# Constant products on TensorE in its first pauses, and a new order of splits, scans and maxima in the first mixer

## The chip, the cores and the metric

The kernel runs on one core of one Trainium2 chip. The metric is the device time of one execution in microseconds (us); the median of three runs of the kernel before is 1240.11 us.

## What is computed

The reference passes 256 rows of width 1024 through two blocks of two layers each, all in fp32. The change touches the first mixer of the first layer alone:

```python
z = xn @ w_in                              # 256 x 2048: q, k, v, u, 512 columns each
q = partial_rope(q) * 64 ** -0.5; k = partial_rope(k)      # 8 heads of 64
att = dilated_attention(q, k, v)           # causal, three dilated windows joined
bu = einsum('gpc,bsgc->bsgp', b_bar, u)    # S5: complex state input,
h = scan(h[t] = a_bar * h[t-1] + bu[t])    # scan over the 256 rows,
y = einsum('gcp,bsgp->bsgc', c, h).real + d * u            # output and skip
ssm = gelu(y) * sigmoid(gelu(y) @ w_glu)
out = concatenate([att, ssm]) @ w_out
```

Behind it follow a feed-forward layer, a gated recurrence with its own, then a latent attention and a grouped attention, each with attention to a memory and a feed-forward layer.

## The kernel before, in words

**Products.** Every fp32 operand of a large product is split into a rounded part and the rest, both fp32r: "hi" is a rounding copy on ScalarE, "lo" a subtraction on VectorE, and a product is hi·hi + hi·lo + lo·hi, three 128x512 matmuls (`mm3`, lines 484 to 486). Transposes are products with the identity (line 490).

**Weights.** All weights come as chunks of 128x2048 (1 MB) in the order of their use. SP's queue loads them into three raw slots (line 2778; a load waits for the lo split of the chunk three before it). `feed(c)` on ScalarE (split at line 1199) and on VectorE (line 1838) splits the chunks up to c + 3; the split tiles have three slots too, so ScalarE's split of a chunk waits until TensorE has used the chunk three before it. Chunks 0 and 1 are u, 2 and 3 q, 4 and 5 k, 6 and 7 v, 8 the first of the output projection, 9 the GLU, 10 to 12 the rest of the output projection.

**The first edge.** x comes in two row tiles of 512 KB. SP issues the first tile, the identity, chunk 0 in quarters, the second tile, chunks 1 and 2, then the S5 tables (BC with B in one layout, C into YG, B in another layout into BB) and the attention's mask (cbias). TensorE waits for the identity and the first tile, turns it (`turn(0, 0)`), and `first_edge` makes the u products: row tile 0 against the quarters of chunk 0 as they come (lines 529 to 539), the turn of tile 1 in between, then `edge_product` (lines 518 to 521) for tile 1 and for chunk 1. ScalarE and VectorE write the turned tiles as hi and rest (VectorE line 1855).

**The middle.** `rows_mm` runs q, k and v, eight k steps of six matmuls each; its argument `at` names what is put behind a step. `u_turn`, `q_turn`, `k_turn` turn u, q and k; `b_turn` turns B; `b_u(q)` (line 753) makes the state input of block q of four, `c_h(q)` (lines 765 to 774) the output of block q from the products W of scan q, `direct_terms` a small table. VectorE runs, for each block, `rotate` (lines 2198 to 2205, the state input times cosine and sine tables and two subtractions), `scan` (two scans, line 2215, then two products W, lines 2219 and 2220, that `c_h` waits for), `skip` (line 2185) and a `table` step (line 2176), after `late_b` (from line 2153) and `late_c` (from line 2163), which form coefficients; GpSimd forms further ones (from line 2693) as soon as `late_c` is done, and `c_h(0)` waits for them. VectorE's order is written out by hand, with a `feed` between these steps.

**The attention.** `attention0` on TensorE makes the scores of heads 0 and 1, then `c_h(3)`, then goes through the heads: scores of head h + 2 (line 801), the turned exponentials of head h (line 490), the product with V of head h - 1 (line 826). Scores of head h + 2 wait for the maxima of head h, which VectorE makes (line 2281; it also adds the mask), the turn for ScalarE's exponentials (line 1524). Ahead of the first exponential ScalarE copies V (`evac_in`) and runs `feed` for chunk 10. The first product with V waits for `skip(2)`. VectorE puts the feeds of chunks 8, 9 and 10 between the maxima of the heads.

Of the kernel before, what the change touches and what calls it, by code (L numbers as in the profile page):

```python
# [8 lines left out]
NR = 3  # L9
# [211 lines left out]
class Tally:  # L221
# [12 lines left out]
    fills half fin turn hthi htlo x yg sq var rs hi2 rowsq hsq  # L234
# [21 lines left out]
def program(nc, A, PLAN, NCH):  # L256
# [10 lines left out]
    with top:  # L267
# [214 lines left out]
        def pe(e):  # L482
# [39 lines left out]

            def first_edge():

                for i in range(4):
                    w = slice(512 * i, 512 * i + 512)
                    e.wait_ge(S.hthi, htlo_n(0, 0, i))
                    e.wait_ge(S.hi, i + 1)
                    e.matmul(PS[:, 0, :], HTh[:, i, 0:128], WH[:, 0, w], start=i == 0, stop=False)
                    e.wait_ge(S.htlo, htlo_n(0, 0, i))  # L530
                    e.matmul(PS[:, 0, :], HTl[:, i, 0:128], WH[:, 0, w], start=False, stop=False)
                    if i == 1:
                        e.wait_ge(S.c_x1, 16)
                        turn(0, 1, (0,))
                    elif i == 3:
                        turn(0, 1, (1,))
                for i in range(4):
                    e.wait_ge(S.lo, i + 1)
                    e.matmul(PS[:, 0, :], HTh[:, i, 0:128], WL[:, 0, 512 * i:512 * i + 512], start=False, stop=False)
                for k in range(4):  # L540
                    tk = edge_product(0, 0, PS[:, 1, :], 1, k, slice(512 * k, 512 * k + 512))
                tk.then_inc(S.used, 1)
                for t in range(2):
                    for k in range(4, 8):
                        if t == 0 and k == 4:
                            e.wait_ge(S.lo1, 1)
                        elif t == 0 and k == 6:
                            e.wait_ge(S.lo, 5)
                        tk = edge_product(0, 1, PS[:, t, :], t, k, slice(512 * k - 2048, 512 * k - 1536))
                tk.then_inc(S.used, 1)  # L550
# [242 lines left out]
            def attention0():  # L793
# [45 lines left out]
                c_h(3)  # L839
                for h in range(9):  # L840
                    if h + 2 < 8:
                        products(h + 2)
                    if h < 8:
                        turn_p(h)
                    if h:
                        pv(h - 1)
                    if h == 5:
                        finish(0)
# [79 lines left out]

            e.wait_ge(S.c_id, 16)
            e.wait_ge(S.c_x0, 16)  # L930
            turn(0, 0)
            first_edge()
# [262 lines left out]
        def act(e):  # L1195
# [288 lines left out]
            feed(PLAN["ev_u"][1])  # L1484
# [348 lines left out]
        def dve(e):  # L1833
# [257 lines left out]
            pd = Tally()  # L2091
            e.wait_ge(S.pa, PA["DT"])
# [66 lines left out]
            def late_c(then):  # L2159
# [6 lines left out]
                then()  # L2166
# [41 lines left out]
            def scan(q):  # L2208
# [5 lines left out]
                for r in range(2):  # L2214
                    e.tensor_tensor_scan(flat(Gq[:, r, :, :]), flat(RT[:, 4 * q:4 * q + 4, :]), flat(Gq[:, r, :, :]), 0.0, MUL, ADD).then_inc(S.dv, dv.up())  # L2215
                if q:
                    e.wait_ge(S.ch, q)
                e.wait_ge(S.dv, dv.n)
# [40 lines left out]
            def attention0():  # L2259
                def step(h):  # L2260
                    if h == 2:
                        skip(2)
                        skip(3)
                    elif h == 3:
                        feed(PLAN["ev_k"][1])
                    elif h == 5:
                        feed(PLAN["ev_v"][0])
                    elif h == 8:
                        feed(PLAN["ev_v"][1])

                e.wait_ge(S.c_m, 16)
                for h in range(9):
                    step(h)
                    if h < 8:
                        for t in range(2):
                            n = 128 * (t + 1)
                            if t == 0:
                                e.wait_ge(S.qk, h + 1)
                                if h > 1:
                                    e.wait_ge(S.ex, 2 * (h - 2) + 2)  # L2280
                            e.tensor_tensor_reduce(out=SM0[:, h % 2, t, 0:n], in0=PS[:, h % 2, 256 * t:256 * t + n], in1=cbias[:, t, 0:n],
                                                   scale=-1.0, scalar=3e38, op0=ADD, op1=ALU.min, accum_out=M0[:, h, t:t + 1]).then_inc(S.mx, 1)
# [489 lines left out]
        def sync(e):  # L2772
# [21 lines left out]
            for c in range(NR, NCH):  # L2794
                weights(c)
# [57 lines left out]
```

## Time and profile before

| | |
|---|---|
| three runs | 1239.87, 1240.11 (median), 1241.81 us |
| profiled execution | 1240.0 us; span of its instructions 1238.2 us |
| TensorE (PE) | 99% of the span busy |
| VectorE (DVE) | 75% |
| ScalarE (ACT) | 57% |
| GpSimd (POOL) | 7% |
| weights and other reads | 214.5 MB, 174 GB/s over the span |

A row of the timeline gives the start and the length of an instruction, or of several merged ones, in us from the span's start; matmuls overlap, so the distance between two starts, not the length, is the pace. In brackets stands how long the engine stood idle before it, and for whom.

### The profile page before, as it was taken

Reading aid. Unit: us, or ns where it says so; the run is one execution under the profiler, and the core shown is the slowest. Engines: PE = TensorE matmul, PEld = TensorE weight load, DVE = VectorE, ACT = ScalarE, POOL = GpSimd, SP = SyncE. Lnnn points to the kernel's source line nnn. Section 1 sums busy time; section 2 is a strip of 40 time slices with the busy share of each in tenths; the row PEclk is TensorE's granted clock in tenths of the full one; section 3 lists DMA queues with packets and bytes.
Section 4 is the critical chain, followed back from the end, with each engine's and each line's share of the span. In section 5 each row is a group of like instructions: output and inputs, shape, how many; then the busy total and the mean of one; then the engine's idle time right before and its main releaser. Section 6 shows DMA issues by size and latency. Waiting matters only on the chain.

```text
span 1238.2 us, 16107 instructions
## 1 busy us (share of the span) xinstructions
PE 1225.8 (99%) x6318; PEld 1021.4 (82%) x6318; DVE 928.7 (75%) x1293; ACT 705.9 (57%) x1065; POOL 89.3 (7%) x121
## 2 busy tenths in 40 slices
PE   7999999999999999999999999999999999999998
PEld 6778888888888888888888888888888888888887
DVE  7995767698788766778887756676888785666787
ACT  7765654455898644455687535444456644544452
POOL 2410000000100100000232000000001300000000
PEclk9999999999999999999999999999999999999999
DMA  8344545555554565555554224545455315555452
GB/s 308 106 137 148 188 171 204 187 187 203 192 201 159 197 213 197 174 189 212 183 200 170 69 103 169 205 170 204 170 204 187 132 35 204 204 173 199 172 183 89
DMA packets 32539, 216.63 MB, mean 175 GB/s; under 512 B 3904, under 2 KB 4544, under 8 KB 7376
## 3 DMA queue, kind: packets, MB, share of 16 engines
q1 hardware_dynamic: 30384, 210.32, 48.6%
q0 software_dynamic: 1360, 4.78, 1.2%
q8 instruction: 50, 0.82, 0.3%
q10 hardware_dynamic: 720, 0.50, 0.1%
q14 instruction: 25, 0.20, 0.1%
HBM read 214.54 MB, written 1.05 MB: 174 GB/s over the span
## 4 chain that ended last, share of the span: by engine, by line
PE 93%; DVE 4%; issue 1%; DMA 1%; ACT 0%; SPq 0%; DVEq 0%; ACTq 0%
PE PS L484 26%; PE PS L486 26%; PE PS L485 26%; PE PS L490 6%; PE PS L860 2%; PE PS L884 1%; PE PS L521 1%; PE PS L519 1%; PE PS L518 1%; PE PS L567 1%; PE PS L562 1%; PE PS L561 1%; DVE WL L1838 1%; DVE YG L2215 1%; DMA X<-in_x 1%
## 5 line engine op out<-in xcount | busy, mean ns | idle before, releaser
L1838 DVE TENSOR_TENSOR WL<-RAW,WH 128x2048 fp32r<-128x2048 f32 (+3 forms) x200 | 434.1, 2174 | 182.3 <-ACT WH L1199 182.3
L1199 ACT ACTIVATE WH<-RAW 128x2048 fp32r<-128x2048 f32 (+3 forms) x200 | 364.4, 1824 | 262.2 <-PE PS L486 262.1
L484 PE MATMUL PS<-WH,HTh 128*128 128x512 f32 (+1 forms) x848 | 334.6, 395 | 0.8 <-DVE WL L1838 0.6
L486 PE MATMUL PS<-WH,HTl 128*128 128x512 f32 (+1 forms) x848 | 329.0, 388 | 0.0
L485 PE MATMUL PS<-WL,HTh 128*128 128x512 f32 (+1 forms) x848 | 328.3, 387 | 0.0
L486 PEld LDWEIGHTS PS<-WH,HTl 128*128 128x128 f32 x848 | 159.2, 188 | 33.3
L484 PEld LDWEIGHTS PS<-WH,HTh 128*128 128x128 f32 x848 | 159.4, 188 | 32.7 <-DVE WL L1838 1.7
L485 PEld LDWEIGHTS PS<-WL,HTh 128*128 128x128 f32 x848 | 159.5, 188 | 30.6
L484 PE MATMUL PS<-WH,YAh 128*128 128x512 f32 x354 | 139.9, 395 | 0.1
L486 PE MATMUL PS<-WH,YAl 128*128 128x512 f32 x354 | 138.0, 390 | 0.0
L485 PE MATMUL PS<-WL,YAh 128*128 128x512 f32 x354 | 137.8, 389 | 0.0
L486 PEld LDWEIGHTS PS<-WH,YAl 128*128 128x128 f32 x354 | 66.4, 188 | 14.0
L484 PEld LDWEIGHTS PS<-WH,YAh 128*128 128x128 f32 x354 | 66.5, 188 | 13.7 <-issue 0.5
L485 PEld LDWEIGHTS PS<-WL,YAh 128*128 128x128 f32 x354 | 66.5, 188 | 13.0
L2635 POOL TENSOR_SCALAR st<-st 128x2 f32<-128x2 f32 (+4 forms) x33 | 21.0, 636 | 752.5 <-ACT JK L1237 679.7
L1216 ACT ACTIVATE YAh<-PS 128x512 fp32r<-128x512 f32 x38 | 21.7, 588 | 58.2 <-DVE JK L2027 29.2
L1216 ACT ACTIVATE HTh<-PS,cst 128x128 fp32r<-128x128 f32 (+1 forms) x136 | 38.8, 380 | 21.9 <-PE PS L490 21.9
L1855 DVE SCALAR_TENSOR_TENSOR HTl<-PS,cst,HTh 128x128 fp32r<-128x128 f32 (+1 forms) x136 | 38.7, 351 | 10.7 <-ACT HTh L1216 10.6
L484 PE MATMUL PS<-WH,YBh 128*128 128x512 f32 x112 | 43.9, 392 | 0.0
L486 PE MATMUL PS<-WH,YBl 128*128 128x512 f32 x112 | 43.6, 389 | 0.0
L485 PE MATMUL PS<-WL,YBh 128*128 128x512 f32 x112 | 43.6, 389 | 0.0
L1854 DVE TENSOR_TENSOR HTl<-YG,HTh 128x512 fp32r<-128x512 f32 x64 | 39.8, 683 | 0.0
(446 smaller groups left out, 1737.6 us busy)
## 6 DMA issues: line engine op xcount, KB each, us to landing
RAW<-in_w SPq DMA_DIRECT2D x196, 1024.0 KB, 4.9
BC<-in_rows POOLq DMA_DIRECT2D x4, 512.0 KB, 4.1
YG<-in_mem POOLq DMA_DIRECT2D x4, 512.0 KB, 5.0
X<-in_x SPq DMA_DIRECT2D x2, 512.0 KB, 5.4
RAW<-in_w SPq DMA_DIRECT2D x4, 256.0 KB, 5.7
BC<-in_s SPq DMA_DIRECT2D x1, 512.0 KB, 11.6
YG<-in_s SPq DMA_DIRECT2D x1, 512.0 KB, 11.9
BB<-in_s SPq DMA_DIRECT2D x1, 512.0 KB, 12.5
```

The lines of the kernel that those rows point to most:

```text
L484: e.matmul(out, ah, bh, start=start, stop=False, skip_group_check=joined)
L485: e.matmul(out, ah, bl, start=False, stop=False, skip_group_check=joined)
L486: return e.matmul(out, al, bh, start=False, stop=stop, skip_group_check=joined)
L490: return e.transpose(out, src, ident[0:p, 0:p])
L518: e.matmul(out, HTh[:, k, ts], WH[:, c % NW, w], start=k == 0, stop=False)
L860: tk = e.matmul(PS[:, h % 2, 256 * t:256 * t + 256], q[:, 128 * t:128 * t + 128], k[:, 0:256], start=i == 0, stop=i == len(parts) - 1)
L1199: e.activation(WH[:, c % NW, w], RAW[:, c % NR, w], ACT.Copy).then_inc(S.hi, 1)
L1216: return e.activation(out, src, ACT.Copy, scale=scale)
L1838: e.tensor_tensor(WL[:, c % NW, w], RAW[:, c % NR, w], WH[:, c % NW, w].bitcast(f32), SUB).then_inc(S.lo, 1)
L1854: return e.tensor_tensor(out, src, hi.bitcast(f32), SUB)
L1855: return e.scalar_tensor_tensor(out, src, gain, hi.bitcast(f32), MUL, SUB)
L2635: e.tensor_scalar(st[:, at:at + n], st[:, at:at + n], 1e-6, None, ADD).then_inc(S.var, 1)
```

## The change

It has six parts. TensorE gets 14 products on a constant tile (`idle_products`), nine ahead of the first turn and five behind it; VectorE writes the tile first of all. `first_edge` has a new order: all hi and rest products of tile 0 and chunk 0 ahead of the turn of tile 1, the products with lo later. In the middle the turns, `c_h` and `b_u` move to later steps of q, k and v. `c_h(3)` moves from ahead of the heads to behind the turn of head 2. On VectorE (and for chunks 3 and 4 on ScalarE) each feed moves to an earlier place between the S5 steps; the maxima of heads 0 and 1 go ahead of scan(3), those of head 2 inside it, and the feeds of chunks 8 to 10 go later. SP loads chunks 3 and 4 ahead of C and of the mask.

```diff
+            def idle_products(n):
+                for _ in range(n):
+                    e.matmul(PS[:, 7, :], YBh[:, 0, 0:128], YBh[:, 0:2, :].rearrange("p a b -> p (a b)"), start=True, stop=True)
             def first_edge():
...
+                for k in range(4):
+                    e.wait_ge(S.hi, k + 1)
+                    hi(0, k)
+                    rest(0, k)
+                e.wait_ge(S.c_x1, 16)
+                turn(0, 1)
+                for k in range(4):
+                    e.wait_ge(S.lo, k + 1)
+                    lo(0, k)
+                for k in range(4):
+                    hi(1, k)
+                    lo(1, k)
+                for k in range(4):
+                    tk = rest(1, k)
                 tk.then_inc(S.used, 1)
+                e.wait_ge(S.hi1, 1)
+                for k in range(4, 8):
+                    if k == 6:
+                        e.wait_ge(S.hi, 5)
+                    hi(0, k)
+                    rest(0, k)
+                for k in range(4, 8):
+                    if k == 4:
+                        e.wait_ge(S.lo1, 1)
+                    elif k == 6:
+                        e.wait_ge(S.lo, 5)
+                    lo(0, k)
+                for k in range(4, 8):
+                    hi(1, k)
+                    lo(1, k)
+                for k in range(4, 8):
+                    tk = rest(1, k)
                 tk.then_inc(S.used, 1)
...
                 products(0)
                 products(1)
-                c_h(3)
                 for h in range(9):
...
                         pv(h - 1)
+                    if h == 2:
+                        c_h(3)
                     if h == 5:
                         finish(0)
...
+            e.wait_ge(S.warm, 1)
+            idle_products(9)
             e.wait_ge(S.c_id, 16)
             e.wait_ge(S.c_x0, 16)
             turn(0, 0)
+            idle_products(5)
             first_edge()
...
-            rows_mm(PLAN["ev_q"], 4, 8, 512, HT, (2, 3), at={2: [u_turn, b_turn], 3: [b_first]})
+            rows_mm(PLAN["ev_q"], 4, 8, 512, HT, (2, 3), at={3: [u_turn], 4: [b_turn], 5: [b_first]})
             rows_mm(PLAN["ev_k"], 4, 8, 512, HT, (0, 1), k_free,
-                    at={0: [lambda: b_u(1)], 1: [direct_terms], 4: [lambda: c_h(0)], 6: [lambda: b_u(2)], 7: [lambda: c_h(1)]})
+                    at={0: [lambda: b_u(1)], 1: [direct_terms], 4: [lambda: c_h(0)], 6: [lambda: b_u(2)]})
             rows_mm(PLAN["ev_v"], 4, 8, 512, HT, (2, 3), v_free,
-                    at={0: [lambda: b_u(3)], 3: [q_turn, lambda: c_h(2)], 6: [k_turn]})
+                    at={1: [lambda: c_h(1)], 2: [lambda: b_u(3)], 3: [q_turn], 6: [lambda: c_h(2), k_turn]})
...
+            feed(PLAN["ev_u"][0])
             e.wait_ge(S.rs, RSTD["row0"])
             evac_in("ev_u", (0, 1), Qn)
-            feed(PLAN["ev_u"][0])
             pairs(0, uT, (4, 5))
+            feed(PLAN["ev_u"][1])
             e.wait_ge(S.bet, 1)
...
             table(0)
-            feed(PLAN["ev_u"][1])
...
             pd = Tally()
+            e.memset(YBh[:, 0:2, :].bitcast(f32), 1.0).then_inc(S.warm, 1)
...
             late_b()
+            feed(PLAN["ev_u"][0])
             table(0)
-            late_c(lambda: feed(PLAN["ev_u"][0]))
-            rotate(0, lambda: feed(PLAN["ev_u"][1]))
+            late_c()
+            feed(PLAN["ev_u"][1])
+            rotate(0)
             table(1)
             feed(PLAN["ev_q"][0])
             scan(0)
             rotate(1)
             table(2)
             skip(0)
+            feed(PLAN["ev_q"][1])
             scan(1)
-            feed(PLAN["ev_q"][1])
             rotate(2)
             table(3)
             skip(1)
+            feed(PLAN["ev_k"][0])
             scan(2)
-            feed(PLAN["ev_k"][0])
             rotate(3)
-            scan(3)
+            skip(2)
...
+                maxima(0)
+                maxima(1)
+                scan(3, lambda: maxima(2))
+                maxima(3)
+                maxima(4)
+                skip(3)
+                for h in range(5, 9):
+                    if h == 5:
                         feed(PLAN["ev_k"][1])
-                    elif h == 5:
+                    elif h == 8:
                         feed(PLAN["ev_v"][0])
...
                 gelu_lo()
+                feed(PLAN["ev_v"][1])
...
             e.dma_start(tt[:, :], A["tab"][:, 640:896]).then_inc(S.c_t, 16)
+            weights(3)
             e.dma_start(YG[:, 0, :], A["s5"][:, 2048:3072]).then_inc(S.c_C, 16)
             e.dma_start(BB[:, :, :, :], A["s5"][:, 0:1024].rearrange("p (r q s) -> p r q s", r=2, q=4)).then_inc(S.c_B, 16)
+            weights(4)
             e.dma_start(cbias[:, :, :], A["tab"][:, 128:640].rearrange("p (t k) -> p t k", t=2)).then_inc(S.c_m, 16)
```

In `first_edge`, `hi(t, k)` is one product of the turned hi part of tile t with WH (it waits for that hi part), `lo(t, k)` the same with WL, `rest(t, k)` one of the rest with WH (it waits for the rest). `scan(q, between)` calls `between` after its two scans, ahead of its two products W. `maxima(h)` makes the two maxima of head h, with the waits they had.

## Rows read from the trace of the kernel before

**Rows 1.** the page, part 1: busy us (share of the span) xinstructions

```profile
PE 1225.8 (99%) x6318; PEld 1021.4 (82%) x6318; DVE 928.7 (75%) x1293; ACT 705.9 (57%) x1065; POOL 89.3 (7%) x121
```

**Rows 2.** timeline, TensorE, first output product: start, us, engine, line, what, xcount

```profile
97.44 0.47 PE L484 MATMUL PS<-WH,YAh 128*128 128x512 f32 x1
```

**Rows 3.** waits, TensorE, 0 to 125 us: who <- for whom: total, times, longest

```profile
PE PS L490 <- DMA ident<-in_tab: 5.1, 1, 5.1
PE PS L529 <- ACT WH L1199: 1.0, 1, 1.0
PE PS L484 <- DVE WL L1838: 0.6, 1, 0.6
PE PS L753 <- DVE JK L2199: 0.6, 1, 0.6
```

**Rows 4.** windows, 0 to 10 us; behind the engines PEclk, DMA share, GB/s

```profile
0.00:10.00 10.00, 3.88 (x12) 2.73 (x12) 4.52 (x21) 5.58 (x14) 3.39 (x17) 1.00 0.80 261
```

**Rows 5.** timeline, TensorE, first edge and first Q product

```profile
8.65 0.63 PE L531 MATMUL PS<-WH,HTl 128*128 128x512 f32 x1
9.08 0.63 PE L529 MATMUL PS<-WH,HTh 128*128 128x512 f32 x1
...
14.75 0.39 PE L518 MATMUL PS<-WH,HTh 128*128 128x512 f32 x1
14.97 0.39 PE L519 MATMUL PS<-WL,HTh 128*128 128x512 f32 x1
...
22.91 0.39 PE L484 MATMUL PS<-WH,HTh 128*128 128x512 f32 x1
```

**Rows 6.** the chain of waits, in order of time: x's second half

```profile
3.52 6.87 DMA X<-in_x
```

**Rows 7.** timeline, VectorE, first edge

```profile
13.24 2.15 DVE L1855 SCALAR_TENSOR_TENSOR HTl<-PS,cst,HTh 128x128 fp32r<-128x128 f32 x8
...
18.61 2.28 DVE L1838 TENSOR_TENSOR WL<-RAW,WH 128x2048 fp32r<-128x2048 f32 x1
```

**Rows 8.** timeline, VectorE, 20 to 53 us

```profile
20.81 1.22 DVE L2153 TENSOR_TENSOR YG<-BC,s 128x1024 f32<-128x1024 f32 x1
...
24.41 0.69 DVE L2176 SCALAR_TENSOR_TENSOR TN<-SX,cosT 128x512 f32<-128x512 f32 x1
...
34.96 2.82 DVE L1838 TENSOR_TENSOR WL<-RAW,WH 128x2048 fp32r<-128x2048 f32 x1
37.70 3.22 DVE L2205 TENSOR_TENSOR YG<-YG,JK 128x512 f32<-128x512 f32 x2
...
51.32 1.29 DVE L2205 TENSOR_TENSOR YG<-YG,JK 128x512 f32<-128x512 f32 x2
```

**Rows 9.** the page, part 6: xcount, KB each, us to landing

```profile
YG<-in_s SPq DMA_DIRECT2D x1, 512.0 KB, 11.9
```

**Rows 10.** timeline, ScalarE, V copies and first exponential

```profile
79.48 1.27 ACT L1216 ACTIVATE Vn<-PS,st 128x512 f32<-128x512 f32 x2 [0.74 <-PE PS L486]
...
82.44 0.40 ACT L1524 ACTIVATE Kn<-Qn,A0M 128x128 f32<-128x128 f32 x1
```

**Rows 11.** timeline, TensorE, last V product to third head

```profile
79.05 0.40 PE L486 MATMUL PS<-WH,HTl 128*128 128x512 f32 x1
...
80.24 0.43 PE L765 MATMUL PS<-uT,K 32*32 32x128 f32 x8
...
82.47 0.92 PE L801 MATMUL PS<-KT,QT 64*128 64x128 f32 x4
83.33 0.58 PE L490 MATMUL PS<-ident,Kn 128*128 128x128 f32 x3
83.84 0.92 PE L801 MATMUL PS<-KT,QT 64*128 64x128 f32 x4
...
85.78 0.92 PE L801 MATMUL PS<-KT,QT 64*128 64x128 f32 x4
```

**Rows 12.** timeline, GpSimd, start of its coefficient stage

```profile
31.19 1.05 POOL L2693 TENSOR_TENSOR CFe<-CFo,s 128x512 f32<-128x512 f32 x1 [6.71 <-DVE CFo L2169]
```

More of the change, by code:

```diff
@@ L233 @@
     c_c c_id c_x0 c_x1 c_p c_i c_t c_B c_C c_m c_S c_bc c_tb c_gr c_mem c_o0 c_o1
-    fills half fin turn hthi htlo x yg sq var rs hi2 rowsq hsq
+    warm fills half fin turn hthi htlo x yg sq var rs hi2 rowsq hsq
     rsx th sg an fold yhi ylo
@@ L521, in edge_product @@
                 return e.matmul(out, HTl[:, k, ts], WH[:, c % NW, w], start=False, stop=k == 7)
+            def idle_products(n):
+                for _ in range(n):
+                    e.matmul(PS[:, 7, :], YBh[:, 0, 0:128], YBh[:, 0:2, :].rearrange("p a b -> p (a b)"), start=True, stop=True)
             def first_edge():
[L525 to L536, printed above, removed]
@@ L537, in first_edge, with hi @@
-                for i in range(4):
-                    e.wait_ge(S.lo, i + 1)
-                    e.matmul(PS[:, 0, :], HTh[:, i, 0:128], WL[:, 0, 512 * i:512 * i + 512], start=False, stop=False)
-                for k in range(4):
-                    tk = edge_product(0, 0, PS[:, 1, :], 1, k, slice(512 * k, 512 * k + 512))
-                tk.then_inc(S.used, 1)
[L543 to L549, printed above, removed]
+                def hi(t, k):
+                    ts, w = slice(128 * t, 128 * t + 128), slice(512 * (k % 4), 512 * (k % 4) + 512)
+                    e.wait_ge(S.hthi, htlo_n(0, t, k))
+                    e.matmul(PS[:, t, :], HTh[:, k, ts], WH[:, k // 4, w], start=k == 0, stop=False)
@@ new lines, in lo, with rest @@
+                def lo(t, k):
+                    ts, w = slice(128 * t, 128 * t + 128), slice(512 * (k % 4), 512 * (k % 4) + 512)
+                    return e.matmul(PS[:, t, :], HTh[:, k, ts], WL[:, k // 4, w], start=False, stop=t == 0 and k == 7)
+                def rest(t, k):
+                    ts, w = slice(128 * t, 128 * t + 128), slice(512 * (k % 4), 512 * (k % 4) + 512)
+                    e.wait_ge(S.htlo, htlo_n(0, t, k))
+                    return e.matmul(PS[:, t, :], HTl[:, k, ts], WH[:, k // 4, w], start=False, stop=t == 1 and k == 7)
@@ L2157, in late_b, with late_c @@
                 e.tensor_tensor(AB[:, 1, :, :], AB[:, 1, :, :], CT_[:, 0, :, :], ADD).then_inc(S.pd, pd.up())
-            def late_c(then):
+            def late_c():
                 e.wait_ge(S.c_C, 16)
@@ L2165, in late_c @@
                 e.tensor_tensor(CT_, CC[:, :, :, :], fi, MUL).then_inc(S.pd, pd.up())
-                then()
                 e.wait_ge(S.pd, PD["f2"])
@@ L2206, in rotate, with scan @@
                 rotated[q] = dv.n
-            def scan(q):
+            def scan(q, between=None):
                 Gq, flat = G[:, q % 2, :, :, :], lambda a: a.rearrange("p j t -> p (j t)")
@@ L2215, in scan @@
                     e.tensor_tensor_scan(flat(Gq[:, r, :, :]), flat(RT[:, 4 * q:4 * q + 4, :]), flat(Gq[:, r, :, :]), 0.0, MUL, ADD).then_inc(S.dv, dv.up())
+                scanned = dv.n
+                if between:
+                    between()
                 if q:
                     e.wait_ge(S.ch, q)
-                e.wait_ge(S.dv, dv.n)
+                e.wait_ge(S.dv, scanned)
                 e.tensor_tensor(W[:, 0:2, :, :], Gq, cosT[:, q % 2, :, :].unsqueeze(1).to_broadcast([128, 2, 4, 128]), MUL).then_inc(S.w, 1)
@@ L2259, in attention0, with maxima @@
             def attention0():
[L2260 to L2264, printed above, removed]
+                def maxima(h):
+                    for t in range(2):
+                        n = 128 * (t + 1)
+                        if t == 0:
+                            e.wait_ge(S.qk, h + 1)
+                            if h > 1:
+                                e.wait_ge(S.ex, 2 * (h - 2) + 2)
+                        e.tensor_tensor_reduce(out=SM0[:, h % 2, t, 0:n], in0=PS[:, h % 2, 256 * t:256 * t + n], in1=cbias[:, t, 0:n],
+                                               scale=-1.0, scalar=3e38, op0=ADD, op1=ALU.min, accum_out=M0[:, h, t:t + 1]).then_inc(S.mx, 1)
+                e.wait_ge(S.c_m, 16)
+                maxima(0)
[6 more added lines that the diff above has]
+                    if h == 5:
                         feed(PLAN["ev_k"][1])
-                    elif h == 5:
+                    elif h == 8:
                         feed(PLAN["ev_v"][0])
[L2268 to L2273, printed above, removed]
-                    if h < 8:
[L2275 to L2282, printed above, removed]
+                    if h < 8:
+                        maxima(h)
                     if h == 6:
@@ L2790, in sync @@
             e.dma_start(tt[:, :], A["tab"][:, 640:896]).then_inc(S.c_t, 16)
+            weights(3)
             e.dma_start(YG[:, 0, :], A["s5"][:, 2048:3072]).then_inc(S.c_C, 16)
             e.dma_start(BB[:, :, :, :], A["s5"][:, 0:1024].rearrange("p (r q s) -> p r q s", r=2, q=4)).then_inc(S.c_B, 16)
+            weights(4)
             e.dma_start(cbias[:, :, :], A["tab"][:, 128:640].rearrange("p (t k) -> p t k", t=2)).then_inc(S.c_m, 16)
-            for c in range(NR, NCH):
+            for c in range(5, NCH):
                 weights(c)
```

## The prediction

> **What bounds the kernel now.** I read the page's busy times first, then TensorE's waits in the first 125 us, then the first stretches, then the instructions of the stages that the change touches. TensorE is busy 99% of the span [rows 1], and behind the first mixer it hardly pauses, so a change of the opening is worth what it does to the moment at which TensorE leaves the attention and starts on the output projection: 97.44 us now [rows 2]. Every later stage hangs on that moment and moves with it. Ahead of it TensorE's named waits are short [rows 3]: 5.1 us until the identity has landed, 1.0 us for ScalarE's first rounded quarter, 0.6 us for a split on VectorE (at the first V product), 0.6 us for VectorE to read the fourth block's state input. A busy TensorE is not a fast one, though. The granted clock reads 1.00 in the first 10 us [rows 4], but two 128x512 products there start 0.43 us apart, and from 14.75 us on 0.22 to 0.23 us apart [rows 5]: the first is the pace of 1.2 GHz, the second that of 2.4 GHz. So the first edge runs partly at the lower level and ends where the first Q product starts, at 22.91 us [rows 5].
>
> **The sum's base.** The profiled execution took 1240.0 us, 1.8 us over its span of 1238.2 us; the median of the three runs is 1240.11 us, 0.1 us more. I work against 1240.0. A measurement of this kernel can tell about 0.2%, 2.5 us, from no change.
>
> **Part 1, the constant products and the new first edge.** Nine 128x512 products on a constant are put ahead of the first turn. VectorE's memset of that constant has no row; it costs between nothing and the 0.7 us of a 128x512 instruction with two inputs, and VectorE's first work needs the constants from memory, which land later, so I take nothing. At 0.43 us each the nine take 3.9 us, from about 1.3 to 5.2 us: inside the wait of 5.1 us. Five more fill the wait of 1.0 us: 1.1 us at the higher level, 2.1 us at the lower. I take it that the clock has risen by about 8 us. Bounds: already by the turn at 5.1 us, or no earlier than now.
>
> What follows isn't bound by TensorE alone. x's second half lands at 3.52 + 6.87 = 10.39 us [rows 6], and its place in the queue is unchanged. Until then all eight first products (hi and rest of four k, 8 x 0.23 = 1.8 us) can be done, paced by ScalarE's quarter splits. Then come eight transposes (0.9 us) and 40 products (40 x 0.227 = 9.1 us): 10.4 + 10.0 = 20.4 us, and 0.4 us for the low part of chunk 1, which VectorE finishes near 17.6 us (18.61 less the four rests between, half of 2.15 us [rows 7]): 20.8 us. VectorE's own queue gives the same figure: nothing ahead of its eight rests at 13.24 us changes, and its split of chunk 2, which the first Q product needs, starts at 18.61 us and takes 2.2 us with what overlaps the next [rows 7, 8]: 20.8 us. So the first Q product starts at 20.85 instead of 22.91 us: **gain 2.05 us**, and however early the clock rises, not much more while VectorE holds that split.
>
> **Part 2, splits ahead of scans, and moved blocks.** VectorE's work from 20.8 us is the same in sum; its order decides what is late. Before b_u(0) it now does late_b (20.81 to 24.41 us, 3.6 us [rows 8]), the split of chunk 3 (2.2), a table (0.69, of which 0.6 before the next starts [rows 8]), late_c (four instructions of late_b's shapes, 3.5) and the split of chunk 4 (2.2), with 0.2 us of waiting for ScalarE: done at 33.1 us. TensorE gives it b_u(0) at 20.85 + 36 x 0.227 + 0.9 + 0.8 (two turns) + 2.4 + 0.5 (changes of operand) = 33.6 us, so they meet. From there I take the stretching beside GpSimd's coefficient stage as now: two subtractions took 3.22 us there against 1.29 us later [rows 8]. Rotation, table, split of chunk 5, scan and two products then end at 46.8 us, 1.0 us before TensorE needs them in c_h(0). I find leads of about 1.0 to 1.3 us also at c_h(1), b_u(3) and the split of chunk 7. So the two waits of 0.6 us go [rows 3]: **gain 1.2 us**; what is next is VectorE, 1 us behind. One more change between plain and short fp32 products costs 0.2 us, which some tenths before the second half of V (now hidden in a busy row) cancel.
>
> On SP's queue two weight loads move ahead of C, B and the mask, and wait there for earlier splits. C lands 11.9 us after its issue now [rows 9], with some 4 MB ahead of it; 1 MB more is 3 us more, and VectorE needs it some 6 us later than it lands now. B follows directly and is needed 3 us after C; the mask, behind the second moved load, only in the attention. Free.
>
> **Part 3, the attention's opening.** This is where I see the cost. The last V product issues at 79.05 us, and the first exponential starts at 82.44 us, because ScalarE first copies V from 79.48 us on (1.27 us) and then splits a weight chunk, for which the last V product has to free a tile [rows 10, 11]. The diff leaves that order. TensorE covers the time today: heads 0 and 1 to 80.24, c_h(3) to 82.47, head 2 to 83.33, then the first turned head without a wait [rows 11]. c_h(3) moves behind the third turned head, so the first turned head still comes 4.0 us after the V products, and TensorE stands for about 2.2 us. The moved c_h(3) then takes its 82.47 - 80.24 = 2.23 us among the heads. They run at 85.78 - 83.84 = 1.94 us each [rows 11], of which the scores take 0.86, the turn 0.5 and the product with V the rest; I read that as TensorE's own work, without a pause that could take c_h(3): **cost 2.2 us**. Bounds: 2.2 us, and 1.7 us if half a microsecond of small waits near the last heads absorbs some.
>
> On VectorE the three maxima ahead of scan(3) and inside it cost what they cost now. skip(3) waits for c_h(3), and behind it stand the split of chunk 8 and head 5's maxima, due some 3.2 us after c_h(3) ends (the split 2.2 us, the rest 1.0); TensorE needs them two heads, 3.9 us, after it, so nothing. The split of chunk 10 goes behind the last divide; its products come after two chunks of the output projection: nothing.
>
> **Sum:** 1240.0 - 2.05 - 1.2 + 2.2 = 1238.95; I forecast 1238.9 us. Bounds: the start 1.6 (that split half a microsecond later) to 2.4 (TensorE's own 20.4 us holds); the waits 0.8 (VectorE takes a third back) to 1.5 (with the tenths before V); the pause 1.7 to 2.2. That makes the forecast's own range 1237.8 to 1239.8.
>
> **Rivals.**
> *The pause is filled (1236.7 us).* If c_h(3) fell into time in which TensorE otherwise stands, the 2.2 us would not be paid. For: VectorE's maxima come earlier than now. Against: the first exponential hangs on ScalarE, whose queue is the same, and the heads run at TensorE's own pace.
>
> *The constant products don't raise the clock early (1240.4 us).* The pace is now seen to have risen by 14.75 us [rows 5], after nearly 10 us of work with pauses in it. If it rose no sooner, five constant products take 2.1 us, the first eight 3.4 us, and the turn begins at 12.4 instead of 10.4 us and runs slowly: ScalarE's copies come 1.5 us or more later, the split of chunk 2 ends near 22.3, and the start's gain is 0.5 us. In the Trainium skill, "TensorE: Matmul & The Clock Gate", Part 1, the slow state is the default and activity lifts it, at a moment that shifts from run to run; by that, this rival's time could come in one run and the forecast's in another. A single profile can't show the shift.
>
> *VectorE falls behind GpSimd (1241.6 us, slower than before).* The two subtractions of rotate(0) lost 1.93 us beside GpSimd, and a split 2.82 against 2.28 us, some 0.5 us [rows 7, 8]. In the new order the split of chunk 4, the subtractions and the table all lie in GpSimd's coefficient stage, which starts with an instruction of 1.05 us [rows 12]. If split and table lose as much as the subtractions, 3.7 us are added; TensorE's lead is 1.0 us, so it stands 2.7 us at c_h(0), and 1238.9 + 2.7 = 1241.6. It decides from 1.0 us of added stretch, and the whole change loses from 2.1 us. In the Trainium skill, "SBUF — State Buffer", "Who interferes with whom", a VectorE instruction with two SBUF inputs and a GpSimd instruction that reads SBUF exclude each other, whichever starts second standing still. The 3.22 us agrees with that, and by that rule every such instruction of the new order may stand once. Against: the same two-input split lay there before and lost 0.5 us.
>
> **Chances.** Forecast 0.52; pause filled 0.18; clock 0.12; VectorE behind 0.18. Below 1237.6 us lies the filled pause and a little of the forecast: 0.20. Above 1242.6 us lies the bad third of the last rival: 0.07. The rest, 0.73, is within 0.2%. The range takes in the clock's rival, most of the filled pause and half of the last: 1236.5 to 1241.3.
>
> **What would show it.** Right: products 0.22 to 0.23 us apart before 10.4 us; first Q product near 20.85 us; no wait at the first V product and at b_u(3); a wait of about 2 us for ScalarE's exponential at the first turned head; output projection at about 96.4 us. Wrong: a first Q product after 22 us (clock); waits of c_h for VectorE's products (VectorE behind); the first turned head less than 3.5 us after the last V product, or heads that take c_h(3) without growing (pause filled).

## The result, and the profile after

The changed kernel takes 1244.86 us in the median of 16 runs (1239.83 to 1245.09), the kernel before 1240.28 us beside it: a ratio of 1.0027, 95% interval 1.0019 to 1.0036. That is 4.6 us slower; I had forecast 1238.9 us, within 0.2% of before, and given 0.07 to slower. One split in these runs matters for everything below: 14 of the 16 took 1243.37 to 1245.09 us at a mean granted clock of 0.995 to 0.997, and two took 1239.83 and 1240.01 us at 1.000. The profiled execution is one of the 14: 1244.86 us, span 1242.9 us. No profile of one of the two was taken.

The page of the changed kernel, part 1 (the row that answers to [rows 1]) and the granted clock by 40 slices of 31 us:

```profile
PE 1233.9 (99%) x6332; PEld 1025.9 (83%) x6332; DVE 930.8 (75%) x1294; ACT 705.5 (57%) x1065; POOL 95.4 (8%) x121
...
PEclk9989999999999999999999999999999999999999
```

TensorE is still busy 99% of the span, but busy for 8.1 us more, with 14 instructions more (the constant products, 5.6 us). The busy share hides the loss; the 8 in the third slice, 62 to 93 us, gives it away.

The waits of TensorE, 0 to 125 us, changed kernel (they answer to [rows 3]):

```profile
PE PS L526 <- DVE YBh L2122: 1.4, 1, 1.4
PE PS L490 <- ACT Kn L1554: 1.2, 2, 1.0
PE PS L827 <- DVE A0M L2302: 0.8, 1, 0.8
...
```

The 5.1, the 1.0 and both 0.6 us of [rows 3] are gone, as forecast. New are the constant (1.4), two waits in the attention, 0.8 us for VectorE's maxima and 1.0 us for ScalarE's first exponential, and three of 0.2 to 0.3 us for splits.

The timeline of TensorE in the first edge, changed kernel (answers to [rows 5]):

```profile
1.44 4.21 PE L526 MATMUL PS<-YBh 128*128 128x512 f32 x9 [1.44 <-DVE YBh L2122]
...
6.39 1.40 PE L526 MATMUL PS<-YBh 128*128 128x512 f32 x5
...
8.28 0.40 PE L542 MATMUL PS<-WH,HTl 128*128 128x512 f32 x1
8.52 0.45 PE L533 MATMUL PS<-WH,HTh 128*128 128x512 f32 x1
...
17.77 0.73 PE L537 MATMUL PS<-WL,HTh 128*128 128x512 f32 x2 [0.29 <-DVE WL L1868]
...
21.09 0.41 PE L484 MATMUL PS<-WH,HTh 128*128 128x512 f32 x1
```

The last row is the first Q product: 21.09 us, against 22.91 us [rows 5]. At 8.28 us the products already follow each other after 0.24 us.

The timelines around the first block's state output, changed kernel, VectorE (answers to [rows 8]) and TensorE:

```profile
36.14 2.32 DVE L2235 TENSOR_TENSOR YG<-YG,JK 128x512 f32<-128x512 f32 x2
38.39 1.53 DVE L2206 SCALAR_TENSOR_TENSOR TN<-SX,cosT 128x512 f32<-128x512 f32 x1
39.84 3.37 DVE L1868 TENSOR_TENSOR WL<-RAW,WH 128x2048 fp32r<-128x2048 f32 x1
...
46.95 1.34 DVE L2253 TENSOR_TENSOR W<-YG,SX 128x1024 f32<-128x1024 f32 x1
```

```profile
47.86 0.40 PE L800 MATMUL PS<-W,CFe 128*32 128x127 f32 x8
48.35 0.43 PE L798 MATMUL PS<-W,CFo 128*32 128x128 f32 x8
```

The subtractions got shorter (2.32 against 3.22 us), but the table now takes 1.53 instead of 0.69 us and the split of chunk 5 takes 3.37 instead of about 2.3 us, beside GpSimd's coefficient stage, which runs from 31.04 to 41.07 us. The second product of the scan ends at 48.29 us. TensorE's groups of eight in this stage start 0.22 us apart; here one starts 0.49 us behind the last: 0.27 us of waiting that the view of waits doesn't name.

The timelines at the attention's opening, changed kernel, ScalarE (answers to [rows 10]) and TensorE (answers to [rows 2, 11]):

```profile
78.14 1.91 ACT L1229 ACTIVATE WH<-RAW 128x2048 fp32r<-128x2048 f32 x1
79.94 0.40 ACT L1554 ACTIVATE Kn<-Qn,A0M 128x128 f32<-128x128 f32 x1
```

```profile
76.55 0.40 PE L486 MATMUL PS<-WH,HTl 128*128 128x512 f32 x1
...
78.66 0.92 PE L827 MATMUL PS<-KT,QT 64*128 64x128 f32 x4 [0.84 <-DVE A0M L2302]
80.58 1.09 PE L490 MATMUL PS<-ident,Kn 128*128 128x128 f32 x3 [1.00 <-ACT Kn L1554]
81.59 1.65 PE L827 MATMUL PS<-KT,QT 64*128 64x128 f32 x4
...
85.17 1.65 PE L827 MATMUL PS<-KT,QT 64*128 64x128 f32 x4
...
88.75 0.65 PE L791 MATMUL PS<-uT,K 32*32 32x128 f32 x8
...
101.75 0.48 PE L484 MATMUL PS<-WH,YAh 128*128 128x512 f32 x1
```

The last V product comes 2.50 us earlier than before (76.55 against 79.05), and the output projection 4.31 us later (101.75 against 97.44). So the loss lies between these two. The pause has come where it was forecast, as two waits of 0.84 and 1.00 us. What I hadn't forecast is behind it: a head takes 85.17 - 81.59 = 3.58 us instead of 1.94 [rows 11]. Windows of the changed kernel (length in us; busy time and instructions of PE, PEld, DVE, ACT, POOL; then PEclk, the mean granted clock, DMA share, GB/s) show why:

```profile
79.00:80.00 1.00, 0.58 (x4) 0.17 (x2) 1.00 (x3) 1.00 (x2) 0.00 (x0) 1.00 0.00 0
80.00:81.00 1.00, 0.33 (x2) 0.17 (x2) 1.00 (x2) 1.00 (x6) 0.00 (x0) 0.92 0.00 0
81.00:82.00 1.00, 1.00 (x4) 0.67 (x5) 1.00 (x6) 1.00 (x6) 0.00 (x0) 0.50 0.00 0
...
90.00:91.00 1.00, 1.00 (x24) 0.94 (x20) 0.00 (x0) 0.00 (x0) 0.00 (x0) 0.50 0.00 0
91.00:92.00 1.00, 1.00 (x40) 0.83 (x32) 0.00 (x0) 0.00 (x0) 0.00 (x0) 0.96 0.00 0
```

The granted clock fell from 1.00 (2.4 GHz) to 0.50 (1.2 GHz) in the window from 80 us and came back in the one from 91 us. A mean of 0.92 is 0.16 us at the lower level, one of 0.96 is 0.08 us, so it was down from about 80.84 to 91.08 us: 10.2 us. Ahead of the fall lie the two waits; behind it TensorE is busy without a pause.

### The profile page after: what moved, and what is told of

Read it like the earlier page. It is cut to its first block, busy times and chain, and to the rows that moved or that the text cites. A ratio compares the mean times of both kernels' runs of the same rounds, so it can differ in the third digit from the quotient of the medians.

```text
span 1242.9 us, 16136 instructions
## 1 busy us (share of the span) xinstructions
PE 1233.9 (99%) x6332; PEld 1025.9 (83%) x6332; DVE 930.8 (75%) x1294; ACT 705.5 (57%) x1065; POOL 95.4 (8%) x121
## 4 chain that ended last, share of the span: by engine, by line
PE 90%; DVE 6%; ACT 1%; issue 1%; POOL 1%; DMA 0%; SPq 0%; DVEq 0%; ACTq 0%
PE PS L484 25%; PE PS L486 25%; PE PS L485 25%; PE PS L490 5%; DVE WL L1868 2%; PE PS L887 2%; PE PS L911 1%; PE PS L521 1%; PE PS L593 1%; PE PS L587 1%; PE PS L588 1%; PE PS L519 1%; PE PS L518 1%; DMA RAW<-in_w 0%; PE PS L852 0%
```

## The experiments

All ratios are to the kernel before, timed beside each kernel. My theory: the pause brings the granted clock down, and that fall is the loss. The rivals put the loss down to other parts of the change, without which the pause would be harmless.

**1. The pause filled.** Seven products of 128x512 whose output nobody reads are added in the changed kernel; the wait ahead of them is for VectorE to have read the bank that they write:

```diff
                 products(1)
+                e.wait_ge(S.ssm, 2)
+                fill_products(3)
                 for h in range(9):
                     if h + 2 < 8:
                         products(h + 2)
+                    if h == 0:
+                        fill_products(4)
```

> The changed kernel with seven more 128x512 products that nobody reads, in the two places where TensorE stands ahead of the first turned head: three behind the scores of heads 0 and 1, four behind the scores of head 2. Nothing else is changed. Theory (the pause there lets the clock fall, and the fall costs 5 us): granted clock 1.000 in all runs, 1239.9 us, as the two runs of the changed kernel without a fall. Rival A (the short fp32 products and c_h among the heads bring the clock down, pause or not): it falls as before, 1244.9 us. Rival B (the early rise by the constant products is what ends near 81 us): falls too, 1244.9 us.

Measured: 1240.35 us (1240.22 to 1240.82, 11 runs, all at clock 1.0), ratio 1.0 (0.9992 to 1.0009). Its timeline of TensorE:

```profile
76.53 0.40 PE L486 MATMUL PS<-WH,HTl 128*128 128x512 f32 x1
...
77.72 0.96 PE L531 MATMUL PS<-HTh 128*128 128x512 f32 x3
...
79.48 1.20 PE L531 MATMUL PS<-HTh 128*128 128x512 f32 x4
80.55 0.84 PE L490 MATMUL PS<-ident,Kn 128*128 128x128 f32 x3
...
97.14 0.48 PE L484 MATMUL PS<-WH,YAh 128*128 128x512 f32 x1
```

The first turned head starts at 80.55 us as in the changed kernel (80.58), so nothing is saved there; but the output projection starts at 97.14 instead of 101.75 us. More work, 4.5 us less time: the fall costs 4.58 us of that stretch (4.61 less 0.03), and without the two waits it doesn't come.

**2. The pause put to use.** The third block's state output, which stood ahead of the last V products, moves into it:

```diff
-  6: [lambda: c_h(2), k_turn]
+  6: [k_turn]
                 products(1)
+                c_h(2)
# VectorE: skip(2) from behind rotate(3) to behind maxima(1)
```

> The changed kernel with c_h(2) moved from behind the seventh step of V to behind the scores of heads 0 and 1, where TensorE stands; skip(2) on VectorE goes behind the maxima of heads 0 and 1. Theory: the V products end 2.2 us earlier, so ScalarE's exponential comes some 1.6 us earlier, TensorE has work in the pause, the clock holds at 1.000, and the time is 1238.3 us. Rival A: the clock falls all the same, some 1243.3 us. Rival B: the same, 1243.3 us.

Measured: 1238.47 us (1237.84 to 1238.85, 11 runs, clock 1.0), ratio 0.9984 (0.9976 to 0.9993). Its timeline of TensorE:

```profile
20.90 0.41 PE L484 MATMUL PS<-WH,HTh 128*128 128x512 f32 x1
...
75.38 0.43 PE L791 MATMUL PS<-uT,K 32*32 32x128 f32 x8
...
78.47 0.58 PE L490 MATMUL PS<-ident,Kn 128*128 128x128 f32 x3
...
95.20 0.47 PE L484 MATMUL PS<-WH,YAh 128*128 128x512 f32 x1
```

No wait is left ahead of the first turned head, and the output projection comes 2.24 us sooner than before. This version beats both kernels: 1.8 us less than before, 6.4 less than the changed kernel.

**3. The pause alone.** In the kernel of before the fourth block's state output is moved as in the change, and nothing else:

```diff
                 products(1)
-                c_h(3)
...
+                    if h == 2:
+                        c_h(3)
# VectorE: skip(3) from h == 2 to h == 4
```

> The kernel before with c_h(3) alone moved behind the third turned head (and skip(3) on VectorE from ahead of head 2's maxima to ahead of head 4's). No constant products, all else as before. Theory: TensorE stands 2.2 us ahead of the first turned head, the clock falls near 84 us in most runs, and the time is 1240.3 + 2.2 + 5.0 = 1247.5 us, with a mean clock near 0.996. Rival B (the early rise is needed for the fall): clock 1.000, 1242.5 us. Rival A: the heads ran without a fall before and still do, so 1242.5 us too, unless c_h(3) among them brings it down from its place on, at 88 us.

Measured: 1247.34 us (1243.18 to 1249.27, 6 runs), ratio 1.0048 (1.0034 to 1.0062); four runs at 0.994 to 0.996, two at 1.000 and 1243.18 and 1243.96 us. The profile is of a run of 1247.38 us; its timeline of TensorE and a window:

```profile
82.54 0.92 PE L801 MATMUL PS<-KT,QT 64*128 64x128 f32 x4 [0.84 <-DVE A0M L2283]
...
84.46 0.83 PE L490 MATMUL PS<-ident,Kn 128*128 128x128 f32 x3 [1.00 <-ACT Kn L1525]
```

```profile
86.00:88.00 2.00, 2.00 (x11) 1.81 (x10) 2.00 (x4) 1.46 (x7) 0.00 (x0) 0.56 0.00 0
```

The same two waits appear, and the granted clock falls in the window from 86 us (0.56 in the mean of two us, so at 86.24 us), reads 0.50 behind it and rises in the one from 93 us (0.97 in one us, so at 93.06 us). So neither the start nor the moved splits are needed for the fall.

That the time came out near the expected 1247.5 us is partly luck. From the last V product to the output projection this profile loses 5.9 us against before (24.26 against 18.39 us). Another 1.4 us are lost ahead of it (last V product at 80.44 against 79.05 us): the first Q product is 0.4 us later, and the granted clock had already read 0.50 from 65.8 to 69.2 us, behind a wait of 0.61 us for the fourth state input that the kernel before has too [rows 3]. The two runs at 1.000 took 0.7 and 1.5 us more than the 1242.5 us expected without a fall; they have no profile.

**4. One wait of two.** Three kernels leave one of the two waits of the changed kernel. In the first, ScalarE splits chunk 10 behind the attention, so that the exponential comes sooner; in the others only one half of experiment 1's products stays.

```diff
             evac_in("ev_v", (2, 3), Vn)
-            feed(PLAN["ev_v"][1])
...
             attention0()
+            feed(PLAN["ev_v"][1])
```

> The changed kernel with ScalarE's split of chunk 10 moved from ahead of the first exponential to behind the attention. Theory: of the pause only the wait for head 0's maxima (0.8 us) and little of the one for the exponential are left; if a pause has to be near 2 us for the fall, the clock holds and the time is 1239.0 us; if 0.9 us is enough, it falls and the time is 1244 us. Rival A: falls, 1244 us. Rival B: falls, 1244 us.

> The changed kernel with four more products in the second of the two waits alone (behind the scores of head 2); the first wait, 0.84 us for VectorE's maxima, stays. If a wait of 0.84 us is short enough to leave the clock up, as in the kernel with the late split, and one of 1.0 us isn't: no fall, clock 1.00, 1240.2 us in every run. Rival: a wait of this length brings the clock down in some runs, wherever it stands: some runs near 1244 us at a clock of 0.996.

> The changed kernel with three more products in the first of the two waits alone (ahead of the scores of head 2); the second wait, 1.0 us for ScalarE's exponential, stays. If it takes both waits to bring the granted clock down: no fall, clock 1.00, and 1240.2 us, like the kernel with both filled. Rival: the second wait, the longer of the two, is enough by itself: a fall to 0.50 behind it, clock 0.996, 1244.9 us.

Measured, with only the 0.84 us left: 1238.92 us (1238.59 to 1239.29, 11 runs) with the late split, ratio 0.9987 (0.9979 to 0.9996), and 1240.41 us (1239.88 to 1240.59, 11 runs), ratio 0.9997 (0.9988 to 1.0006), with four products in the second wait; all 22 runs at clock 1.0. With only the 1.00 us left: 1245.08 us (1240.46 to 1245.47, 7 runs), ratio 1.0031 (1.002 to 1.0041), six of the seven at 0.995 to 0.997. My expectation that it takes both waits was wrong. The kernel with the late split, its timeline, and then the one with only the second wait, its timeline and windows:

```profile
78.63 0.92 PE L827 MATMUL PS<-KT,QT 64*128 64x128 f32 x4 [0.84 <-DVE A0M L2302]
79.48 0.55 PE L490 MATMUL PS<-ident,Kn 128*128 128x128 f32 x3
```

```profile
81.06 0.83 PE L490 MATMUL PS<-ident,Kn 128*128 128x128 f32 x3 [1.00 <-ACT Kn L1561]
```

```profile
82.00:84.00 2.00, 2.00 (x14) 1.55 (x14) 2.00 (x6) 2.00 (x10) 0.00 (x0) 0.89 0.00 0
84.00:86.00 2.00, 2.00 (x7) 1.35 (x8) 1.64 (x8) 1.00 (x5) 0.00 (x0) 0.50 0.00 0
```

The fall comes some 2.5 us behind the end of that wait (0.89 is 0.44 us at the lower level: about 83.56 us against 81.06), while the heads already run without a pause. So the cause of a slow row can be a wait some us ahead of it, with full rows between.

**5. Both repairs.** Experiment 2 and the late split together.

> The changed kernel with both repairs: the third block's state output stands in the pause, and ScalarE's split of chunk 10 goes behind the attention. My theory: in the kernel with the state output moved, the first turned head already has no wait, so the earlier exponential has nothing left to shorten: 1238.4 us, within 0.3 us of 1238.47, clock 1.00. Rival: ScalarE's split also held up the later heads, whose exponentials then come earlier: about 1237.6 us.

Measured: 1238.51 us (1238.04 to 1239.14, 11 runs), ratio 0.9984 (0.9976 to 0.9993). As expected, the second repair has nothing left to shorten.

**6. What brings the clock back.** The moved state output one head earlier in the changed kernel, nothing added:

```diff
-                    if h == 2:
+                    if h == 1:
                         c_h(3)
```

> The changed kernel with the fourth block's state output one head earlier, behind the second turned head. Nothing is added or left out, and both waits ahead of it stay. In three profiles with a fall the level rose while that state output ran (36 products of some 128 columns, two or three times as many in a microsecond as in the heads). If it is this work that brings the level back, the rise comes with it about one slow head, 3.6 us, sooner: the stretch at 0.50 is about 6.8 instead of 10.2 us and the fallen runs take about 1244.9 - 3.4/2 = 1243.2 us, with mean clock 0.997. Rival: the level comes back at its own time whatever runs: the stretch stays at 10.2 us, and the fallen runs at 1244.9 us and 0.996. Runs without a fall: 1240 to 1240.5 us in both.

Measured: 1243.38 us (1241.76 to 1243.97, 10 runs), ratio 1.0024 (1.0014 to 1.0033); eight runs at 0.997, two at 0.999. Its timeline and windows:

```profile
84.72 0.65 PE L791 MATMUL PS<-uT,K 32*32 32x128 f32 x8
```

```profile
78.00:80.00 2.00, 0.92 (x4) 0.52 (x4) 2.00 (x8) 2.00 (x4) 0.00 (x0) 0.99 0.00 0
80.00:82.00 2.00, 1.88 (x6) 1.33 (x7) 2.00 (x6) 2.00 (x10) 0.00 (x0) 0.50 0.00 0
...
84.00:86.00 2.00, 2.00 (x28) 1.45 (x31) 0.32 (x2) 1.07 (x6) 0.00 (x0) 0.50 0.00 0
86.00:88.00 2.00, 2.00 (x57) 1.74 (x50) 0.00 (x0) 0.00 (x0) 0.00 (x0) 0.80 0.03 8
```

The clock was down from about 79.96 to 86.80 us: 6.8 us, as expected, instead of 10.2. The level came back 2.1 us after the state output began, against 2.3 us in the changed kernel (91.08 less 88.75), 1.5 us in experiment 3 and 2.9 us in the kernel with the second wait alone. The time fell by 1.5 us against the changed kernel, where 1.7 was expected. So the heads, once slow, stayed slow until the state output came, and moving it forward shortened the fall. The time from its start to the rise is no constant, and the stretch was 6.8 us in experiment 3 and with the second wait alone as well, so the place alone doesn't set the length.

**7. The opening of before.** The changed kernel with scan, maxima and state output ordered as before:

```diff
             rotate(3)
-            skip(2)
+            scan(3)
...
                 products(1)
+                c_h(3)
```

> The changed kernel with the attention's opening of before: the fourth scan and its products ahead of the maxima, the fourth block's state output behind the scores of heads 0 and 1. By the rows of the changed kernel the rotation ends at 76.98, the scan and both products at about 81.6 us, so the state output, asked for at 77.7 us, starts near 80.5 and the first turned head near 83.7 us, against 80.58 us plus the 2.2 us of the state output that now stands later: 0.9 us more than the undisturbed 1239.9 us, that is 1240.8 us if the clock holds. I expect a fall behind that wait of about 2.8 us, and 1245 to 1246 us. Rival: the state output in its old place fills the wait for ScalarE and the clock stays up: 1238.5 us.

Measured: 1242.48 us (1241.45 to 1255.45, 10 runs), ratio 1.0022 (1.0003 to 1.0042). Three runs at clock 1.000 took 1241.45 to 1241.78, six at 0.999 1242.32 to 1243.06, one 1255.45 us at 0.986. The profile, of a run at 1.000, shows one long wait:

```profile
81.33 0.43 PE L798 MATMUL PS<-W,CFo 128*32 128x128 f32 x8 [2.73 <-DVE W L2251]
```

The wait came as worked out, but I missed on the fall: behind 2.73 us of waiting the clock stays at 1.00 in this profile, and the six runs at 0.999 can have fallen for little. The run of 1255.45 us stays unexplained. Here the state output stands right behind the wait; that this is why, by experiment 6, is argued, since no profile of a run at 0.999 was taken. Putting the old opening back is no repair: VectorE's scan isn't ready for it.

**8. The start.** The new start alone in the kernel of before (its constant, both sets of constant products, the new first edge), for two profiles; and the kernel of experiment 2 without the constant and its fourteen products:

```diff
-            e.wait_ge(S.warm, 1)
-            idle_products(9)
...
-            idle_products(5)
```

> The kernel of before with the new start alone: constant, constant products, new order of the first edge; every later order as before. If the start's gain survives alone, the first Q product comes at about 21.1 us and the time is 1240.3 - 1.8 = 1238.5 us. Rival: VectorE, whose order is that of before, takes the gain back in longer waits at the first V product and the fourth state input (0.6 us each before, then about 1.5 us each): 1240.2 us, and the moved splits are what makes the start's gain count.

> The same kernel as the one with the new start alone, for a second profile; in the first the granted clock fell for 3.4 us behind the wait of 0.59 us at the first state input, and the time was 1240.29 us all the same. If VectorE, not the fall, takes the start's gain back, a profile without a fall shows waits for VectorE of over 1.5 us in sum at the first V product and the fourth state input, and about 1240.5 us. Rival: the fall is what takes it back, and a profile without one gives about 1238.6 us. If the clock falls again, waits for VectorE stay away and nothing is told.

> The changed kernel with the third block's state output in the pause (1238.47 us), without the constant and its fourteen products. Theory: these products are what brings the higher level early; without them the first edge runs at 0.43 us a product up to 10 us and more, the first Q product comes at about 22.6 us, and the time is about 1240.0 us. Rival: the new order of the first edge alone brings the gain: first Q product at about 21.1 us, 1238.5 us.

Measured: the start alone 1240.64 us (1240.21 to 1241.96, 11 runs), ratio 1.0003 (0.9994 to 1.0012), and 1241.15 us in the one run of the second profile. Without the constant products 1239.12 us (1238.55 to 1239.29, 11 runs), ratio 0.9988 (0.9979 to 0.9997). The start alone, timeline and windows:

```profile
29.44 0.72 PE L779 MATMUL PS<-uT,BBe 32*128 32x128 f32 x8 [0.59 <-ACT BBe L1245]
```

```profile
32.00:34.00 2.00, 2.00 (x6) 1.51 (x6) 2.00 (x2) 2.00 (x4) 1.92 (x3) 0.50 0.86 360
34.00:36.00 2.00, 2.00 (x8) 1.58 (x7) 2.00 (x2) 1.97 (x4) 2.00 (x2) 0.65 0.01 4
```

Its first Q product comes at 20.79 us, 2.1 us sooner than before (21.78 us in the second profile), and then TensorE waits for ScalarE at the first state input, 0.59 and 0.61 us; in both profiles the granted clock falls to 0.50 behind the end of that wait, by 2.5 and 2.7 us, and stays there for 3.4 us. Yet six of its runs at clock 1.000 took 1240.21 to 1240.86 us, no less. The gain is lost in either case; that VectorE takes it where the clock holds would need a profile without a fall, and neither is one. It stays open.

The kernel without the constant products, its timeline:

```profile
22.79 0.39 PE L484 MATMUL PS<-WH,HTh 128*128 128x512 f32 x1
...
96.62 0.47 PE L484 MATMUL PS<-WH,YAh 128*128 128x512 f32 x1
```

Its first Q product comes at 22.79 us, against 20.90 with them (experiment 2) and 22.91 before: the products, not the new order of the edge, bring the start forward, by 1.89 us here. The size is that of two profiles; in the eleven profiles with these products the first Q product comes at 20.65 to 21.78 us, in the three without at 22.79 to 23.31 us. But the whole kernel gains only 1239.12 - 1238.47 = 0.65 us by them. At the output projection 1.42 us are left (96.62 against 95.20); of the 0.47 us lost until there VectorE takes 0.30 at the first block's state output, where two groups start 0.52 us apart with them and 0.22 us without. Behind the output projection's start another 0.42 us go (1141.20 against 1140.78 us to the end of the span).

## Why the prediction was wrong

**The failed step is the price in the third part, "cost 2.2 us": it takes the heads behind the pause at "1.94 us each" [rows 11].** Those rows were taken at a granted clock of 1.00. I had named the two levels in the first edge [rows 5] and never asked whether the new pause brings the lower one back. By the mean clock it did so in 14 of 16 runs; in the profiled one a head then took 3.58 us, and the fall cost 4.58 us, none of which is in my bounds of 1.7 to 2.2 us.

The pause itself was forecast rightly, in place and cause. TensorE stands because ScalarE's queue is unchanged, and the first turned head comes 80.58 - 76.55 = 4.03 us behind the last V product, where I had said 4.0. TensorE stands there for 0.84 + 1.00 = 1.84 us, not 2.2, but the term held in sum: from the last V product to the output projection the kernel with the filled pause takes 97.14 - 76.53 = 20.61 us against 18.39 before [rows 2, 11], 2.2 us more.

In the Trainium skill, "TensorE: Matmul & The Clock Gate", "A second HAM failure mode: psum-queue depth-cycling", a kernel is described whose TensorE idles briefly and often between groups of matmuls, so that its clock goes to and fro. The falls behind waits of 0.84 and 1.00 us here agree with that in so far as short idles were enough.

**Part 1, the start:** forecast 20.85, measured 21.09 us, with the wait for the low part of chunk 1 that I had set at 0.4 us measured at 0.29. Gain 1.82 instead of 2.05 us. That it all counts was wrong: in experiment 8 the constant products bring 0.65 us of time. The clock's rival didn't come: the pace was 0.24 us at 8.28 us, and in none of the eleven profiles with the products does the first Q product come after 22 us.

**Part 2, the waits:** both of 0.6 us went, but 0.27 us came at the first block's state output and 0.2 us at a split, so the last V product is 2.50 us earlier: 1.82 + 0.68, where 1.2 was forecast. I took the rest of VectorE's work from rows beside an idle GpSimd; the table and the split took 1.9 us more beside a busy one. So the third rival did come, at a tenth of its price (0.27 instead of 2.7 us): the subtractions gave 0.9 us back, and the lead of 1.0 us took most of the remainder. In the Trainium skill, "SBUF — State Buffer", "Who interferes with whom", any VectorE instruction with two SBUF inputs can stand still beside GpSimd's reads of SBUF, not the subtractions alone. The split's 3.37 us agrees: it starts at 39.84 us, some 1.2 us before GpSimd's last instruction of that stage ends at 41.07 us, and takes 1.1 us more than 2.28.

**The rest of the span** isn't rigid, as I took it: behind the output projection's start the profiled span loses another 0.39 us (4.7 less 4.31). That belongs to the constant products: from there to the end of the span it is 1141.10 to 1141.24 us in all eleven profiles with them and 1140.76 to 1140.90 us in the three without. One row of it is a wait of 0.27 us for a product of VectorE, at 675.88 us in the changed kernel; all eleven have such a wait and none of the three. Why it comes is not known. Outside the span lie 1.96 instead of 1.8 us.

Together, without the fall: -1.82 - 0.68 + 2.2 + 0.39 + 0.16 = +0.25 us against the profiled 1240.0, so 1240.25; the two runs at 1.000 took 1239.83 and 1240.01 us, the filled one 1240.35. With 4.58 us for the fall this is 1244.8, as measured. The terms 0.68, 0.39 and 0.16 are remainders of the same profile, so that the sum closes shows little; the test of the fall's share is the filled kernel, in which the first turned head starts as late and the clock holds. The first rival, a filled pause, did not come in this kernel, where both waits stand; filled with another block, in experiment 2, it gave 1238.47 us instead of the rival's 1236.7.

## What to carry to other kernels

Ask of every new pause of TensorE not only how long it is but whether the granted clock holds behind it: here 1.8 us of waiting cost 4.6 us more in the work that followed, while the busy share stayed at 99%. When a block of work that hid a wait is moved away, look for another block that can stand there (here 6.4 us less than with the pause); if there is none, products that nobody reads were cheaper here than the pause (4.5 us less). A gain at the start counts only as far as the next engine in the chain can follow, so take its prices from rows with the same neighbour busy.

## What the runs showed of the hardware that I had not expected

The granted clock fell behind a single wait of 1.00 us in six of seven runs, with TensorE busy ahead of it and behind it, and held in all 22 runs with a single wait of 0.84 us in the same place. Elsewhere less was enough: it fell behind waits of 0.59 and 0.61 us at the first state input (both profiles of the new start alone) and of 0.61 us at the fourth (experiment 3). Yet it held in the profile with one wait of 2.73 us. So the length of a wait alone doesn't decide, and what does stays open; the same kernel falls in some of its runs and holds in others.

The fall can come late. In experiment 6 it came within the second wait (at 79.96 us, the wait ends at 80.12), in the changed kernel 0.3 us behind it, with the second wait alone 2.5 us behind it. Once down, the clock came back in each profile with slow heads only while the state output ran, 1.5 to 2.9 us after that began.

The kernel before isn't free of falls: of the 21 runs beside experiment 7, four show 0.999 and 1241.39 to 1242.37 us, the other 17 show 1.000 and at most 1240.88. The fall at the fourth state input in experiment 3 is a likely place for them, since the kernel before has that wait; no profile of such a run shows it.
